# Delta rule, turn and gated sum as one program ordered by keys

## The chip, the cores and the metric

The kernel runs on one core of one Trainium2 chip. The metric is device time in microseconds (us) for one launch. The core's engines are TensorE (PE in the profile, PEld its weight loads), VectorE (DVE), ScalarE (ACT), GpSimd (POOL) and SyncE (SP), which issues most transfers; each works through its own list of instructions in order and waits on semaphores.

## What is computed

One step of a hybrid decoder layer for 512 prompt tokens and 8 sample tokens that share the weights. The part in question, cut from the reference:

```python
proj = einsum('btd,df->btf', u, w_in)            # u = rmsnorm(x)
o_nsa, o_mem = ...                               # two attention mixers
o_gdn, s_new = gated_delta_chunked(q, k, v, g, beta, s0)
o_gdn = rmsnorm(o_gdn, o_norm) * silu(z)
gates = sigmoid(g_br)                            # g_br: 3 x 1024 columns of u @ w_in
merged = (gates[:, :, 0] * (o_nsa @ w_br_nsa)
          + gates[:, :, 1] * (o_gdn @ w_br_gdn)
          + gates[:, :, 2] * (o_mem @ w_br_mem))
h = x + merged @ w_out
y = h + square(relu(rmsnorm(h) @ w_ff1)) @ w_ff2
```

For a sample token the delta rule is one step on a 128x128 state per head and sequence (32 states): read k·S and q·S, form the new value, and S becomes e^g·S + k·v'.

## The kernel before

The kernel is a list of stages, `stages()`. Each is one block in which every engine gets its instructions; at a block's end the engines meet at a barrier. Semaphores made with `local_sem` are cleared and freed between stages (`retire`, L222) with a further barrier; those made with `sem` live to the end. The last stages are:

- `stage_gdn_sample`: the sample tokens' delta rule. SP loads the 32 states (`s_S`, 2 MB) and the first two weight tiles. DVE and PE go through a chain: norms of q and k (L2350 to L2364), 32 small products that read the states (L2318, each shows as two matmuls of 2 columns), new value `s_vn` and result `s_oT` (L2371 to L2377), two transposes to rows (L2321, L2322), four of the result (L2325), then the norm and gate of the result into `proj` (L2382 to L2389). The states' update is eight products of 512 columns (L2331); DVE scales a quarter head pair (L2393) and adds the product (L2395). SP stores the states and waits for the stores.
- `stage_turn`: the three mixers' results, in `proj` by tokens, are turned to channels by PE (L2441, 15 groups of four transposes) and split by DVE into a high part `oH` and a low part `oL` (`high_low`, L298 and L300), so that one fp32 product is three float32r products. SP loads back the input `u` as `uH` and `uL` (2 MB each).
- `stage_merge`: 12 pairs of weight tiles of 256 columns. A gate tile (1024 rows, 1 MB) gives four units of 24 matmuls, whose sum ACT takes through a sigmoid (L2512) into `sig`. The branch tile that follows it (512 rows, 0.5 MB) gives four units of 12 matmuls, which DVE multiplies with `sig` (L2527) and, from the second branch on, adds to `mergedT` (L2532, L2534); in the last four pairs it also splits the sum (L298, L300). Gate units take turns in PSUM banks 0 to 3, branch units in 4 to 7. DVE splits every tile, `split_tile`, as soon as PE has done the tile two before it; two buffers each for raw, high and low weights. At its end it splits the first two tiles of `w_out`, and SP loads `h` (the input x, 2 MB).
- `stage_out_ffn`: output product with `w_out` (four tiles, units of 24 matmuls over token tiles, added to `h` at L2735), norm, and the feed-forward network (L329 under L2588). A unit waits until the sum of the unit four before it is taken from its bank.

All products go through `product3` (L329), so this line is that of most matmuls. `by_key` merges several generators into one list of instructions: each yields a number before a piece of code, and the piece with the lowest number is written next. It sets the order on an engine; what is waited for is set by the semaphores.

Of the kernel before, what the change touches and what calls it, by code (L numbers as in the profile page):

```python
# [69 lines left out]
def rows(t):  # L70
    return P if t < TT else NB
# [98 lines left out]
class Kernel:  # L170
# [73 lines left out]
    def build(self):  # L244
        nc = self.nc
        with self.stack:
# [17 lines left out]
            self.vecs_loaded = self.sem("vecs_loaded")  # L264
            stages = self.stages()
# [441 lines left out]
    def stage_inputs(self):  # L707
# [81 lines left out]
        self.beta, self.g = self.sb("beta", [P, TT + 1, GH]), self.sb("g", [P, TT + 1, GH])  # L789
# [715 lines left out]
    def stage_prompt_mixers(self):  # L1505
# [14 lines left out]
        self.cTs = self.sb_high("cTs", [P, CC, NB])  # L1520
# [749 lines left out]
    def stage_gdn_sample(self):  # L2270

        nc, I, O, ps, proj = self.nc, self.I, self.O, self.ps, self.proj
        ident, cTs = self.C("ident"), self.cTs
        HB = GH * NB
        S0 = self.sb("s_S0", [P, GH, NB, P])
        self.wt = [self.sb(f"wt{i}", [P, KC, WCOLS]) for i in range(2)]
        sq, qkn = self.sb("s_sq", [P, 2 * HB]), self.sb("s_qkn", [P, 2 * HB])
        rn = self.sb("s_rn", [P, 2 * HB])
        pairs = self.sb("s_pairs", [P, HB, 2])
        prod = self.sb("s_prod", [P, HB])  # L2280
        gb = self.sb("s_gb", [NB, 2, HB])
        bcs = self.sb("s_bcs", [P, 3, HB])
        vn, oT = self.sb("s_vn", [P, HB]), self.sb("s_oT", [P, HB])
        rows_kv = self.sb("s_rows", [HB, 2, P])
        Vm = self.sb("s_Vm", [HB, HB, P])
        eg = self.sb("s_eg", [NB, GH])
        tmp = self.sb("s_tmp", [P, HB])
        so, sqo = self.sb("s_so", [NB, GH]), self.sb("s_sqo", [NB, GH, GD])
        S = self.sem
        s_in, stored = S("s_in"), S("s_stored")  # L2290
        p = Steps(S("s_pe"), ["sums", "bc", "qk", "read", "rows", "orow"] + [f"add{i}" for i in range(8)])
        a = Steps(S("s_act"), ["eg", "rt", "rows", "sqo", "ro"])
        v = Steps(S("s_dve"), ["sq", "mean", "gb", "prod", "pairs", "vn", "oT", "Vm", "so", "out"] + [f"add{i}" for i in range(8)])
        two = lambda x: x.rearrange("p c b -> p (c b)")
        with nc.Block() as block:
            @block.sync
            def _(sp):
                for h in range(GH):
                    sp.dma_start(S0[:, h], I["state_gdn"][:, h].rearrange("b k v -> k b v")).then_inc(s_in, 16)
                for srcs, chunks in self.merge_tiles()[0:2]:  # L2300
                    self.load_tile(sp, srcs, chunks)
                for h in range(GH):
                    v.wait(sp, f"add{2 * h + 1}", 0)
                    sp.dma_start(O["s_state"][:, h].rearrange("b k v -> k b v"), S0[:, h]).then_inc(stored, 16)
                sp.wait_ge(stored, 64)

            @block.tensor
            def _(pe):
                v.wait(pe, "sq", 0)
                p.done(pe.matmul(ps[:, 0, 0:2 * HB], self.C("ones"), sq[:, :], start=True, stop=True), "sums", 0)  # L2310
                v.wait(pe, "gb", 0)
                p.done(pe.matmul(ps[:, 1, 0:2 * HB], self.C("ones")[0:NB, :], gb.rearrange("b i c -> b (i c)"), start=True, stop=True), "bc", 0)
                v.wait(pe, "prod", 0)
                p.done(pe.matmul(ps[:, 2, 0:HB], self.C("ones"), prod[:, :], start=True, stop=True), "qk", 0)
                v.wait(pe, "pairs", 0)
                pe.wait_ge(s_in, 64)
                for i in range(HB):
                    ins = pe.matmul(ps[:, 3, 2 * i:2 * i + 2], S0[:, i // NB, i % NB, :], pairs[:, i, :], start=True, stop=True)  # L2318
                p.done(ins, "read", 0)
                v.wait(pe, "vn", 0)  # L2320
                pe.transpose(ps[0:HB, 4, 0:P], qkn[:, HB:], ident)  # L2321
                p.done(pe.transpose(ps[0:HB, 4, P:2 * P], vn[:, :], ident), "rows", 0)  # L2322
                v.wait(pe, "oT", 0)
                for h in range(GH):
                    ins = pe.transpose(ps[0:NB, 5, h * P:(h + 1) * P], oT[:, h * NB:(h + 1) * NB], ident)  # L2325
                p.done(ins, "orow", 0)
                v.wait(pe, "Vm", 0)
                for i in range(8):
                    if i >= 2:
                        v.wait(pe, f"add{i - 2}", 0)  # L2330
                    p.done(pe.matmul(ps[:, 6 + i % 2, :], rows_kv[:, 0, :], Vm[:, 4 * i:4 * i + 4, :], start=True, stop=True), f"add{i}", 0)  # L2331

            @block.scalar
            def _(act):
                a.done(act.activation(eg[:, :], self.g[0:NB, TT, :], ACT.Exp), "eg", 0)
                v.wait(act, "mean", 0)
                a.done(act.activation(rn[:, :], rn[:, :], ACT.Sqrt), "rt", 0)
                p.wait(act, "rows", 0)
# [513 lines left out]
```

## Time and profile before

| | us |
|---|---|
| median of 3 runs | 1685.5 (1683.55 to 1691.86) |
| the profiled execution, its own time | 1689.1 |
| span of that execution | 1687.2 |
| PE, PEld, DVE, ACT, POOL busy | 1472.1, 1348.7, 880.0, 374.7, 82.0 |
| mean granted TensorE clock, share of full speed | 0.907 |

The profile is of one execution, whose own time stands beside its span. Times in its rows are microseconds from the span's start, and a row that ends in `[idle before <-releaser]` tells how long the engine had done nothing and what ended that. The three stages that the change joins reach from 950.4 to 1241.3.

### The profile page before, as it was taken

The numbers are of one execution on the slowest core, as the hardware profiler recorded it, in microseconds if no ns is written. First come the engines' busy times: TensorE is split into PE (matmuls) and PEld (weight loads), VectorE is DVE, ScalarE is ACT, GpSimd is POOL, SyncE is SP. The second block draws the span as 40 slices with busy tenths as digits, with TensorE's granted clock in tenths as the row PEclk, the third lists the DMA queues.
The fourth block names the chain that finished last, engine by engine and source line by source line (L and its number), as shares of the span: only waits on it lengthen the run. The fifth ranks groups of instructions, "written<-read, shape, count | busy, mean of one in ns | idle before, by whom it ended". The sixth has DMA issues, their size and how long they took to land. (4 is left out here: it accounts for less than half of the span.)

```text
span 1687.2 us, 27010 instructions
## 1 busy us (share of the span) xinstructions
PE 1472.1 (87%) x11343; PEld 1348.7 (80%) x11343; DVE 880.0 (52%) x1598; ACT 374.7 (22%) x874; POOL 82.0 (5%) x76
## 2 busy tenths in 40 slices
PE   6999899879878788988556567999989999999998
PEld 5778789879877677867344447999979999999998
DVE  3554257658434556654233264445654746555563
ACT  3543033223314344544122100010003101000000
POOL 0000001100011111110000000000000000000000
PEclk8999999989958798988678658999989999999999
DMA  9231125142401000000754342332341233233231
GB/s 342 87 131 59 50 79 179 51 175 79 132 10 51 0 1 1 1 1 8 302 204 156 97 149 77 92 96 77 99 164 38 75 101 100 79 97 99 75 101 51
DMA packets 115649, 159.03 MB, mean 94 GB/s; under 512 B 6040, under 2 KB 106840, under 8 KB 112779
## 3 DMA queue, kind: packets, MB, share of 16 engines
q1 hardware_dynamic: 111886, 122.76, 22.7%
q0 software_dynamic: 2304, 33.56, 4.9%
q8 instruction: 84, 1.38, 0.4%
q10 hardware_dynamic: 1348, 1.12, 0.2%
q14 instruction: 27, 0.21, 0.0%
HBM read 145.04 MB, written 16.66 MB: 96 GB/s over the span
## 5 line engine op out<-in xcount | busy, mean ns | idle before, releaser
L329 PE MATMUL ps<-uH,wh 128*128 128x260 f32 x576 | 165.5, 287 | 21.3 <-DVE wl L300 12.4
L298 DVE CAST wh<-wt 128x2048 fp32r<-128x2048 f32 (+1 forms) x75 | 85.7, 1143 | 128.7 <-PE ps L329 101.0
L329 PE MATMUL ps<-hH,wh 128*128 128x260 f32 x512 | 145.6, 284 | 2.6 <-DVE hT L300 2.6
L329 PE MATMUL ps<-mergedH,wh 128*128 128x260 f32 x512 | 145.5, 284 | 0.0
L329 PE MATMUL ps<-hH,wl 128*128 128x260 f32 x512 | 145.5, 284 | 0.0
L329 PE MATMUL ps<-hT,wh 128*128 128x260 f32 x512 | 144.8, 283 | 0.0
L329 PE MATMUL ps<-mergedH,wl 128*128 128x260 f32 x512 | 144.6, 282 | 0.0
L329 PE MATMUL ps<-mergedT,wh 128*128 128x260 f32 x512 | 144.6, 282 | 0.0
L456 PE MATMUL ps<-XT,w 128*128 128x256 f32 (+1 forms) x512 | 125.7, 387 | 6.3 <-DVE XT L519 6.0
L329 PEld LDWEIGHTS ps<-uH,wh 128*128 128x128 f32 x576 | 110.6, 192 | 21.6 <-issue 12.5
L300 DVE TENSOR_TENSOR wl<-wt,wh 128x2048 fp32r<-128x2048 f32 (+1 forms) x58 | 120.2, 2072 | 2.0
L329 PE MATMUL ps<-uL,wh 128*128 128x260 f32 x384 | 109.7, 286 | 0.0
L329 PE MATMUL ps<-uH,wl 128*128 128x260 f32 x384 | 109.6, 285 | 0.0
L456 PEld LDWEIGHTS ps<-XT,w 128*128 128x128 f32 x512 | 92.8, 192 | 19.1 <-DVE XT L519 7.4
L329 PEld LDWEIGHTS ps<-hH,wh 128*128 128x128 f32 x512 | 97.2, 190 | 2.8 <-DVE hT L300 2.8
L329 PEld LDWEIGHTS ps<-hT,wh 128*128 128x128 f32 x512 | 97.1, 190 | 0.0
L329 PEld LDWEIGHTS ps<-hH,wl 128*128 128x128 f32 x512 | 97.0, 189 | 0.0
L329 PEld LDWEIGHTS ps<-mergedH,wh 128*128 128x128 f32 x512 | 96.4, 188 | 0.0
L329 PEld LDWEIGHTS ps<-mergedH,wl 128*128 128x128 f32 x512 | 96.4, 188 | 0.0
L329 PEld LDWEIGHTS ps<-mergedT,wh 128*128 128x128 f32 x512 | 96.4, 188 | 0.0
L2721 ACT ACTIVATE positive<-ps 128x260 f32<-128x260 f32 x64 | 24.9, 389 | 300.7 <-PE ps L329 300.7
L329 PE MATMUL ps<-wh,uH 128*128 128x256 f32 (+1 forms) x304 | 87.8, 289 | 0.0
(517 smaller groups left out, 3427.3 us busy)
## 6 DMA issues: line engine op xcount, KB each, us to landing
wt<-in_w_ff SPq DMA_DIRECT2D x32, 1024.0 KB, 5.3
wt<-in_w_in SPq DMA_DIRECT2D x27, 1024.0 KB, 5.4
ring<-in_cache_mem_kv SPq DMA_DIRECT2D x4, 2048.0 KB, 25.1
w<-in_cmp_w SPq DMA_DIRECT2D x8, 512.0 KB, 7.8
ring<-in_cache_win_kv SPq DMA_DIRECT2D x2, 2048.0 KB, 19.5
wt<-in_w_out SPq DMA_DIRECT2D x4, 1024.0 KB, 6.1
out_s_win<-in_cache_win_kv SPq DMA_DIRECT2D x1, 4088.0 KB
scratch_uhigh<-uH SPq DMA_DIRECT2D x1, 2080.0 KB
```

The lines of the kernel that those rows point to most:

```text
L298: dve.tensor_copy(high, x).then_inc(high_sem, 1)
L300: return dve.tensor_tensor(low, x, high.bitcast(F32), ALU.subtract)
L329: ins = pe.matmul(out, lhsT(i, c), rhs(j, c), start=(first and c == 0 and k == 0), stop=(last and c == chunks - 1 and k == 2))
L456: return pe.matmul(out, self.w1[:, v, J * r + j, :], x, start=(i == 0), stop=(i == 2 * J - 1))
L2721: act.activation(positive[:, k % 4, :], ps[:, k % 4, 0:HALF], ACT.Relu).then_inc(relu, 1)
```

## The change

`stage_gdn_sample`, `stage_turn` and `stage_merge` become one block, `stage_tail`, whose five lists are written with `by_key`. What it does:

- The order of tiles is gate 0, gate 1, then branch q and gate q + 2 in turn; it ends gate 11, branch 10, branch 11. `sig` holds two tiles. Gate units have banks 0 and 1, branch units 2 to 4, early turns 2 to 5, the delta rule 6 and 7.
- 14 of the 15 groups of transposes stand ahead of the first product or right behind it; the sample rows of the delta rule's mixer, which need its result, come in the third gate tile. ACT now makes `oH`, DVE makes `oL`.
- The small products, transposes and state updates of the delta rule stand between units. `Vm` is made in eight parts of 512 columns instead of one of 4096.
- SP issues the first weight tile, `uH`, `uL`, the second tile, the states, then the rest. Three raw buffers; the low part of a tile is written over its raw part, so tile n is loaded when tile n - 3 is done.
- `h` is loaded, and the second tile of `w_out` split, at the start of `stage_out_ffn`. The new stage's semaphores are local, so that `retire` stands behind it.

```diff
-    def stage_turn(self): ...
-    def stage_merge(self): ...
+    def stage_tail(self):
...
+        seq = [("gate", 0), ("gate", 1)]
+        for q in range(Q):
+            seq += [("branch", q)] + ([("gate", q + 2)] if q + 2 < Q else [])
...
+        START = 13.0
+        start = [START]
+        for kind, _ in seq:
+            start.append(start[-1] + NU * (2.87 if kind == "gate" else 1.44))
+        unit_at = lambda n, i: start[n] + i * (start[n + 1] - start[n]) / NU
...
+        turns = [(br, t) for br in range(3) for t in range(TT)] + [(0, TT), (2, TT), (1, TT)]
+        EARLY = len(turns) - 1
+        turn_key = lambda i: 1.5 + 1.1 * i if i < EARLY else 47.0
...
+        add_key = lambda i: 49.0 + 6.0 * i
...
+                def load(n):
...
+                    if n >= 3:
+                        sp.wait_ge(self.w_split, k - 1)
+                        sp.wait_ge(acc, self.tile_end[k - 3])
...
+                def loads():
...
+                    load(0)
+                    for x, dram in zip((self.uH, self.uL), self.u_dram):
+                        sp.dma_start(x.bitcast(F32)[:, :, :], dram).then_inc(u_back, 16)
+                    load(1)
+                    for h in range(GH):
+                        sp.dma_start(S0[:, h], I["state_gdn"][:, h].rearrange("b k v -> k b v")).then_inc(s_in, 16)
...
+                            if kind == "gate":
+                                if u >= 2:
+                                    pe.wait_ge(gated, u - 1)
+                                out, rhs, chunks = ps[:, u % 2, 0:HALF], lambda i, c: X[i][:, c, tok], KC
+                            else:
+                                if u >= 3:
+                                    pe.wait_ge(taken, u - 2)
+                                out, rhs, chunks = ps[:, 2 + u % 3, 0:HALF], lambda i, c: O3[i][:, q // BP, c, tok], 4
...
+                    for i in range(HB):
+                        if i % 8 == 0:
+                            yield 26.0 + 3.0 * (i // 8)
...
+                    for i in range(8):
+                        yield add_key(i) + 1.0
...
+                def splits():
+                    yield 6.5
+                    split(0)
+                    for n in range(1, NT_ + 1):
+                        yield start[n - 1] + 0.2
+                        split(n)
...
     def stage_out_ffn(self):
...
+                sp.dma_start(h[:, 0:TT, :], I["x_prompt"][0].rearrange("(t p) d -> p t d", p=P)).then_inc(h_in, 16)
+                sp.dma_start(h[0:NB, TT, :], I["x_sample"][:, 0, :]).then_inc(h_in, 16)
...
+                self.high_low(dve, self.last_raw, self.wh[k % 2], wlow[k % 2], self.w_high, k + 1).then_inc(self.w_split, 1)
...
-                dve.wait_ge(self.h_in, 32)
+                dve.wait_ge(h_in, 32)
```

Where it moves instructions, first on PE at the start of the joined stages, as far as the first product. Before (`s_S` are the states, `proj` the results to be turned, `consts` the identity or ones, UNCONDITIONAL_BRANCH a block's edge):

```order
L2310 MATMUL ps<-s_sq_9120,consts_49 128x64
L2312 MATMUL ps<-s_gb_9125,consts_49 128x64
L2314 MATMUL ps<-s_prod_9124,consts_49 128x32
L2318 MATMUL ps<-s_pairs_9123,s_S_127_9117 128x2 x32
...
L2325 MATMUL ps<-consts_49,s_oT_9128 8x128 x4
L2331 MATMUL ps<-s_Vm_9130,s_rows_9129 128x512 x8
L2295 UNCONDITIONAL_BRANCH
L2433 UNCONDITIONAL_BRANCH
L2441 MATMUL ps<-consts_49,proj_1644 128x128 x16
...
L329 MATMUL ps<-uH_9336,wh_154_9491 128x260
```

With the change (`temps` are the delta rule's small tiles), with the first unit's 24 matmuls cut short:

```order
L2447 MATMUL ps<-temps_9141,consts_49 128x64
L2440 MATMUL ps<-consts_49,proj_1647 128x128 x4
L2450 MATMUL ps<-temps_9141,consts_49 128x64
L2440 MATMUL ps<-consts_49,proj_1647 128x128 x4
L2453 MATMUL ps<-temps_9141,consts_49 128x32
L2440 MATMUL ps<-consts_49,proj_1647 128x128 x36
L330 MATMUL ps<-uH_9122,wh_144_9134 128x260
...
L2440 MATMUL ps<-consts_49,proj_1647 128x128 x4
L2440 MATMUL ps<-consts_49,proj_1647 128x8 x8
...
L2460 MATMUL ps<-temps_9141,s_S_135_9125 128x2 x8
```

The state reads and updates now stand behind the first product, between units; 11 groups of transposes stand ahead of it, one full and two small groups behind its first unit.

On SP at the same place, before and then with the change:

```order
L2299 DMA s_S_127_9117<-in_state_gdn 128x8x128 x4
L291 DMA wt_128_9118<-in_w_in 128x8x256
L291 DMA wt_129_9119<-in_w_br_nsa 128x4x256
L2304 DMA out_s_state<-s_S_127_9117 128x8x128 x4
L2295 UNCONDITIONAL_BRANCH
L2428 UNCONDITIONAL_BRANCH
L2431 DMA uH_9336<-scratch_uhigh 128x4160
L2431 DMA uL_9337<-scratch_ulow 128x4160
```

```order
L2375 DMA tw_136_9126<-in_w_in 128x8x256
L2382 DMA uH_9122<-scratch_uhigh 128x4160
L2382 DMA uL_9124<-scratch_ulow 128x4160
L2375 DMA tw_137_9127<-in_w_in 128x8x256
L2385 DMA s_S_135_9125<-in_state_gdn 128x8x128 x4
L2375 DMA tw_138_9128<-in_w_br_nsa 128x4x256
```

`uH` and `uL` moved from behind the stores of the states to behind one weight tile, and the states behind both.

On DVE from the end of the joined stages into the next, before:

```order
L298 CAST mergedH_9500<-mergedT_9498 128x260
L300 TENSOR_TENSOR mergedT_9501<-mergedT_9498,mergedH_9500 128x260
L298 CAST wh_156_9493<-wt_129_9119 128x2048
L300 TENSOR_TENSOR wl_160_9497<-wt_129_9119,wh_156_9493 128x2048
L2476 UNCONDITIONAL_BRANCH
L2723 UNCONDITIONAL_BRANCH
L2748 MEMSET ss_12007 128x15
L298 CAST woH_174_11999<-wt_128_9118 128x2048
```

With the change:

```order
L299 CAST mergedH_9139<-mergedT_9138 128x260
L301 TENSOR_TENSOR mergedT_9140<-mergedT_9138,mergedH_9139 128x260
L2364 UNCONDITIONAL_BRANCH
L2839 UNCONDITIONAL_BRANCH
L299 CAST wh_145_9135<-tw_137_9127 128x2048
L301 TENSOR_TENSOR tw_140_9130<-tw_137_9127,wh_145_9135 128x2048
L2868 MEMSET ss_12007 128x15
L299 CAST woH_163_11999<-wt_154_11990 128x2048
```

The second `w_out` tile's split moved from ahead of the block's edge to behind it. `h` and the third `w_out` tile are now issued behind the same edge.

## Rows read from the trace of the kernel before

**Rows 1.** The page, part 1: busy time of each engine, share of the span.

```profile
PE 1472.1 (87%) x11343; PEld 1348.7 (80%) x11343; DVE 880.0 (52%) x1598; ACT 374.7 (22%) x874; POOL 82.0 (5%) x76
```

**Rows 2.** Windows: stretch, its length, busy us of each engine, granted clock, DMA share, GB/s.

```profile
950.40:1023.10 72.70, 40.51 (x152) 28.11 (x153) 41.42 (x74) 4.18 (x7) 0.00 (x0) 0.55 0.43 138
1023.10:1236.00 212.90, 210.13 (x1728) 209.94 (x1728) 104.82 (x157) 18.63 (x48) 0.00 (x0) 0.99 0.33 102
```

**Rows 3.** Timeline of PE, next stage: start, us, engine, line, operation, idle before.

```profile
1241.31 0.55 PE L329 MATMUL ps<-wh,mergedH 128*128 128x256 f32 x1 [8.06 <-PEq L2476]
```

**Rows 4.** Timeline of PE, delta rule to first product, same columns.

```profile
960.92 13.78 PE L2318 MATMUL ps<-s_pairs,s_S 128*128 128x2 f32 x64 [6.71 <-DMA s_S<-in_state_gdn]
...
976.19 1.01 PE L2325 MATMUL ps<-consts,s_oT 128*8 128x128 f32 x4
...
985.71 10.60 PE L2331 MATMUL ps<-s_Vm,s_rows 32*128 32x512 f32 x12 [0.91 <-DVE s_S L2395]
...
1008.96 0.66 PE L2441 MATMUL ps<-consts,proj 128*128 128x128 f32 x4 [0.55 <-DVE oL L300]
...
1023.12 0.56 PE L329 MATMUL ps<-uH,wh 128*128 128x260 f32 x1 [12.42 <-DVE wl L300]
```

**Rows 5.** Transfers issued from 940 to 1060: KB each, us to landing.

```profile
wt<-in_w_in SPq DMA_DIRECT2D x4, 1024.0 KB, 5.3
...
uL<-scratch_ulow SPq DMA_DIRECT2D x1, 2080.0 KB, 13.9
```

**Rows 6.** Windows of 2 us in the turn stage, columns of rows 2.

```profile
1004.00:1006.00 2.00, 2.00 (x19) 1.75 (x19) 1.97 (x4) 0.00 (x0) 0.00 (x0) 0.98 0.98 416
1012.00:1014.00 2.00, 0.00 (x0) 0.00 (x0) 1.90 (x6) 0.00 (x0) 0.00 (x0) 0.50 0.16 67
```

**Rows 7.** Timeline of SP, where the turn stage issues its transfers.

```profile
1000.71 0.34 SPq L2431 DMA_DIRECT2D uH<-scratch_uhigh  x1
```

**Rows 8.** Timeline of DVE in the last pair of tiles and at the next stage's start.

```profile
1220.13 0.69 DVE L298 CAST wh<-wt 128x1024 fp32r<-128x1024 f32 x1
1220.85 1.23 DVE L300 TENSOR_TENSOR wl<-wt,wh 128x1024 fp32r<-128x1024 f32 x1
...
1231.06 0.42 DVE L2532 TENSOR_TENSOR m_prod<-ps,sig 128x260 f32<-128x260 f32 x1
1231.51 0.43 DVE L2534 TENSOR_TENSOR mergedT<-mergedT,m_prod 128x260 f32<-128x260 f32 x1
1231.98 0.30 DVE L298 CAST mergedH<-mergedT 128x260 fp32r<-128x260 f32 x1
1232.31 0.43 DVE L300 TENSOR_TENSOR mergedT<-mergedT,mergedH 128x260 fp32r<-128x260 f32 x1
...
1237.44 1.22 DVE L298 CAST wh<-wt 128x2048 fp32r<-128x2048 f32 x1
1238.69 2.29 DVE L300 TENSOR_TENSOR wl<-wt,wh 128x2048 fp32r<-128x2048 f32 x1
...
1248.19 1.23 DVE L298 CAST woH<-wt 128x2048 fp32r<-128x2048 f32 x1 [6.78 <-DMA wt<-in_w_out]
```

**Rows 9.** Timeline of ACT over the joined stages, same columns.

```profile
950.68 1.28 ACT L2337 ACT_TABLE_LOAD   x1
951.98 0.26 ACT L2337 ACTIVATE s_rn<-s_rn 128x64 f32<-128x64 f32 x1
...
1028.43 0.39 ACT L2512 ACTIVATE sig<-ps 128x260 f32<-128x260 f32 x1 [7.85 <-PE ps L329]
...
1227.52 0.39 ACT L2512 ACTIVATE sig<-ps 128x260 f32<-128x260 f32 x1 [2.50 <-PE ps L329]
```

**Rows 10.** Timeline of DVE, first operation behind a stage whose semaphores are local.

```profile
950.48 0.23 DVE L2350 TENSOR_TENSOR s_sq<-cTs 128x64 f32<-128x64 f32 x1 [1.37 <-PEq L222]
```

**Rows 11.** Windows of 2 us in the next stage, columns of rows 2.

```profile
1310.00:1312.00 2.00, 0.61 (x6) 0.40 (x4) 1.97 (x2) 0.39 (x1) 1.35 (x1) 1.00 0.00 0
1316.00:1318.00 2.00, 2.00 (x11) 2.00 (x10) 1.93 (x5) 0.37 (x1) 0.00 (x0) 0.50 0.09 26
```

More of the change, by code:

```diff
@@ new lines, in loads @@
+                def loads():
+                    yield 0.0
+                    load(0)
[4 more added lines that the diff above has]
+                        sp.dma_start(S0[:, h], I["state_gdn"][:, h].rearrange("b k v -> k b v")).then_inc(s_in, 16)
+                    for n in range(2, len(tiles)):
+                        yield start[n - 2] if n >= 3 else 0.1
+                        if n == 2:
+                            sp.wait_ge(self.w_split, k0 + 1)
+                        load(n)
@@ new lines, in turn @@
+                def turn():
+                    for i, (br, t) in enumerate(turns):
+                        yield turn_key(i)
+                        if i == EARLY:
+                            v.wait(pe, "out", 0)
+                            pe.wait_ge(oL_kept, EARLY)
+                        elif i >= 4:
+                            pe.wait_ge(oL_kept, i - 3)
+                        if (br, t) == (2, TT):
+                            pe.wait_ge(self.mem_back, 16 * MH)
+                        for c in range(4):
+                            ins = pe.transpose(ps[:, turn_bank(i), c * P:c * P + rows(t)], proj[0:rows(t), t, cols[br] + c * P:cols[br] + (c + 1) * P],
+                                               ident[0:rows(t), 0:rows(t)])
+                        ins.then_inc(turned, 1)
@@ new lines, in dense @@
+                def dense():
+                    for n, (kind, q) in enumerate(seq):
+                        if kind == "gate":
+                            continue
+                        for i, (m, tok) in enumerate(U):
+                            yield unit_at(n, i + 1) + 0.1
+                            u = NU * q + i
+                            dst, high, lo = (x[:, WM * (q % BP) + m, tok] for x in (self.mergedT, self.mergedH, self.mergedL))
+                            dve.wait_ge(gated, u + 1)
+                            dve.wait_ge(acc, acc_of("branch", q, i))
+                            if u == 0:
+                                dve.wait_ge(turned, EARLY)
+                            x, y = ps[:, 2 + u % 3, 0:HALF], sig[:, q % 2, m, tok]
+                            if q < BP:
+                                dve.tensor_tensor(dst, x, y, ALU.mult).then_inc(taken, 1)
+                                continue
+                            e = u - BP * NU
+                            if e >= 2:
+                                dve.wait_ge(added, e - 1)
+                            dve.tensor_tensor(prod2[:, e % 2, :], x, y, ALU.mult).then_inc(taken, 1)
+                            dve.wait_ge(taken, u + 1)
+                            dve.tensor_tensor(dst, dst, prod2[:, e % 2, :], ALU.add).then_inc(added, 1)
+                            if q >= 2 * BP:
+                                dve.wait_ge(added, e + 1)
+                                self.split_acts(dve, dst, high, lo)
@@ new lines, in _ @@
+                by_key(splits(), dense(), turn(), sample())
+                dve.wait_ge(self.x_split.sem, self.x_split.n)
+        self.issued, self.splits = k0 + NT_ + 2, k0 + NT_ + 1
+        low_of = {(k0 + NT_ + i) % 2: (NT_ + i) % 3 for i in range(2)}
+        third = (NT_ + 2) % 3
+        self.wl = [low[low_of[i]] for i in range(2)]
+        for i in range(2):
+            self.taken[f"wl{i}"] = self.taken.pop(f"tw{low_of[i]}")
+        self.last_raw = raw[(NT_ + 1) % 3]
+        self.taken["wt0"] = self.taken.pop(f"tw{third}")
```

477 lines of the change are left out of this document (242 added, 235 removed).

## Prediction

> **What bounds the kernel now.** I read the page's table of engines first: PE is busy for 1472.1 of 1687.2 us, DVE for 880.0, so the end moves only if time in which PE has no useful work goes [rows 1]. Then windows by stage. From 1023.1 to 1236.0, the gated sum, PE is busy for 210.1 of 212.9 us at a clock of 0.99: full, 1728 matmuls of 0.122 us. From 950.4 to 1023.1, delta rule and turn, it is busy for 40.5 of 72.7 us at 0.55, near the lower of its two levels (1.2 of 2.4 GHz) [rows 2]; ahead of the next stage's first product, at 1241.31, it stands for 8.06 [rows 3]. The timeline shows what those 72.7 us are: a wait for the states, 13.8 us of state reads at half clock, the updates, then transposes that wait for DVE, and 12.4 us in which PE waits for DVE's last splits, until the first product at 1023.12 [rows 4]. That product needs `uH`, `uL` and one split weight tile. None of the delta rule is needed before the second branch, so the stretch is a queue of things that stand ahead of the product only by the order of stages.
>
> **The start.** S is 950.4. The first product now waits for the later of two things.
> - Transfers. Before, `uL` landed 13.9 us after it was issued [rows 5]; the traffic of it and `uH` (4.26 MB) ran at 416 GB/s and had almost ended at 1012.4, 11.7 us after the first issue at 1000.7 [rows 6, 7]. Now one tile of 1.05 MB goes ahead, 2.5 us at 416 GB/s. So 11.7 + 2.5 = 14.2 at the low end, and 0.4 + 13.9 + 2.5 + 0.7 = 17.5 at the high end. I take 16, the middle.
> - DVE and the transposes. The first tile lands at about 5.3 [rows 5]. DVE by then has the short chain of norms (some 4 us) and four turns; it splits at 7.5 to 11 (3.5 us [rows 8]) and turns 4 to 7 follow. The 11th group of transposes needs DVE's seventh turn, so PE is through at about 13.5. ACT's half of a turn runs beside DVE's. This hides under the transfers by 2.5 us; without them it would set the start.
>
> The first product moves from S + 72.7 to S + 16: **56.7 us gained**. The slow clock of its first unit (ended 5.3 us after it began, where units at full clock take 24 x 0.12 = 2.9 [rows 4, 9]) is paid as before.
>
> **What PE gets in between.** It is PE time on the path now, but at full clock, at which a matmul pitch is half.
> - State reads: 13.8 us at 0.50 [rows 4], so 6.9 at full clock; upper bound 13.8.
> - Updates: 12 matmuls, six products, took 10.6, 1.77 each; eight at half of that are 7.1; upper bound 14.1.
> - Transposes of the new value and the result: 1.01 at half clock for four [rows 4], six now: 0.8.
> - The turn groups behind the first product: one full, 0.66 at full clock [rows 4], and three of 8 columns, which I bound by 0 and 0.66 and take as 0.4: 1.9.
>
> Sum **16.7 us lost**, up to 32 if none of it speeds up.
>
> Waits in between: the two transposes to rows stand behind the third unit of branch 0 (4.3 us after its begin). DVE must by then have split gate 2 (3.5), taken a unit (0.43) and made `vn` (0.7): 4.6. So PE waits 0.3. The late turn stands two gate units (5.8) behind the result's transposes; DVE's chain there is a unit 0.4, a small split 1.9, the reduce 0.8, the root 0.2, norm and gate 2.3: 5.6, hidden by 0.2 to 0.7. The eight updates add 16 us of DVE work over some 50 us in which DVE was busy for half; PE's third unit ahead is the cover (three branch banks), and by my walk through the list a unit's bank is free 0.3 us before it is wanted. If that cover goes, each branch tile waits what DVE is late.
>
> ACT now loads tables twice more, between the result's transposes and the third gate tile's first sigmoid. The row shows 1.28 us per load, and the operation behind it starts 0.02 us after its end [rows 9]. The chain square 0.6, load, root at 3.4, load, sigmoid ends at 5.1 after branch 0; PE wants that bank at 6.2. Hidden: 0. The Trainium skill ("ScalarE: Activation LUTs", What ACT_TABLE_LOAD costs) counts a drain of about 1380 ns beside the load's 1283, 2.66 us per switch of set; by that the sigmoid would end at 7.1 and PE would wait 0.9 us. The rows have no such drain, so the sum goes by them.
>
> **The end of the stage.** After the last gate tile there are now two branch tiles. DVE's list from there: a small split 1.9 (0.69 + 1.23), four units of 1.6, a full split 3.5, four units of 1.6 [rows 8]: 18.2 us, against PE's 11.6; DVE ends it. Then 0.4 to the next stage, and 1.0 more since the semaphores are now local: the one such place shows 1.37 us idle [rows 10], where this edge took 0.3 to 0.4 [rows 3, 8]. Together 19.6. Before, from the last gate unit's end at 1227.5 [rows 9] to 1241.3 [rows 3] it was 13.8, with one branch tile. The other tile's 48 matmuls (5.8) have left the part ahead, so the end costs 19.6 - 5.8 = 13.8: **0**. PE's idle time moves, it doesn't go.
>
> **The next stage.** DVE starts with a split of 3.5 us, then waits for `h`, which was loaded long before and is now issued here, 2.1 MB ahead of the third `w_out` tile. That tile was split at 1248.19, 6.9 us behind the edge [rows 3, 8]; 2.1 MB at 416 GB/s add up to 5, so its split begins at 10 to 11.8 and the first sum leaves its bank at 14 to 15.8. PE has four banks: ramp and four units are 2.4 + 4 x 2.85 = 13.8. So it waits 0 to 2 us; **1 lost**. The 16 splits of `oH` that went to ACT and the rest of DVE's savings lie beside PE: 0.
>
> **Sum.** 56.7 - 16.7 - 0.3 - 0 - 1 = 38.7 us. On this execution's own 1689.1 that is 1650.4; it was 3.6 us above the median of the runs, and on the median of 1685.5 it is 1646.8. I forecast **1647 us**.
>
> **Rivals.**
> 1. *The start comes later.* The second tile (1.05 MB) and the states (2.1 MB) are issued right behind `uL` and share the engines. With all 8.5 MB at 300 to 416 GB/s before the last piece of `uL` lands, the first product is at S + 26. For it: `uL` landed 2.6 us after the traffic's end. Against it: `uH` and `uL` ran at nearly full share of the engines, and what is issued first mostly lands first. 10 us less gain: **1657**. Chance 0.14.
> 2. *The pieces between units stay dear.* Each switch from product to small matmul and back waits for a semaphore, and the reads keep their half-clock price: 15 us less, **1662**. For it: only rows at the low clock show them. Against it: the transposes at 0.66 for four ran at full clock within a stretch of small ones. Chance 0.09.
> 3. *Slower: the clock.* PE stood for some 2.6 us around 1312, and by 1316 its granted clock was 0.50 [rows 11]; a fall costs 2.4 us as in the first unit. Gate units have two banks instead of four, branch units three. If PE stands that long at the 23 tile edges, it pays 55 us: 1647 + 55 = **1702**. It decides from 16 falls (38.7 / 2.4). Against it: a sigmoid takes 0.39 us and has a whole unit of 2.9 us of cover, and a split of 3.5 us has a tile of 5.8. Chance 0.03. The Trainium skill ("TensorE: Matmul & The Clock Gate", A second HAM failure mode: psum-queue depth-cycling) says that small idle times between groups of matmuls, from cycling through PSUM banks, make the clock fall and rise again and again. By that rule the result would be this rival's; the trace of before, at 0.99 over the gated sum, does not show it with four banks.
> 4. *The change doesn't do what it says*: some wait in one of the five lists keeps the product behind the delta rule, and only the store wait and the stage edges go, some 8 us: 1678. Chance 0.02.
>
> **Numbers.** My forecast has 0.72 (own range 1640 to 1653: start 14.2 to 17.5, next stage 0 to 2, runs of before 6 us apart). Rivals 0.14, 0.09, 0.03, 0.02. The range 1640 to 1660 holds most of the forecast, rival 1 and part of rival 2, some 0.82. A measurement can tell about 0.5%, 8.4 us, from no change. Faster by more: forecast, rivals 1 and 2, 0.95; within: 0.02; slower: 0.03.
>
> **What would show it.** The first product with `uH` 16 us after the first small matmul of the delta rule; state reads of some 1.7 us for eight; updates of 0.9 us; a clock of 0.98 or more from there to the last gate tile; PE idle for 6 to 8 us at the edge; `h` and the third `w_out` tile landing 10 us behind it. Wrong: a first product later than S + 20, idle times of PE over 1 us at tile edges, or a clock under 0.95 in the gated sum.

## The result and the profile after

The changed kernel takes 1650.17 us in the median of 4 runs (1644.59 to 1651.61), the kernel before beside it 1688.68 (4 runs). The ratio is 0.977, with an interval of 0.9743 to 0.9796: 38.5 us less. The forecast was 1647, the range 1640 to 1660. In a later set of six executions the ratio was 0.9782 (0.9748 to 0.9817). One execution of the combined version further down, at 2105.31 us and a granted clock of 0.637, was in a slower state of the chip and is left out of its median.

The page's table of engines, of the changed kernel's profiled execution (own time 1644.59, span 1642.8, clock 0.929):

```profile
PE 1453.0 (88%) x11343; PEld 1335.0 (81%) x11343; DVE 871.7 (53%) x1590; ACT 384.5 (23%) x891; POOL 82.1 (5%) x76
```

PE has the same 11343 matmuls as in [rows 1] and is busy for 19.1 us less. Of these, 12.6 lie in the joined stages (250.6 to 238.1), where work of the slow clock now runs at the fast one, and 5.8 lie ahead of them, in code that is the same. The span is 44.4 us shorter, so the other 25.3 were idle time of PE. But 44.4 is more than the change gives, as a cut of each execution at three marks shows: the first DVE operation of the joined stages (S), the next stage's first product, and the end.

| us | before S | S to next stage's first product | from there to the end |
|---|---|---|---|
| before | 950.5 | 290.8 | 445.9 |
| changed | 942.9 | 252.8 | 447.1 |
| changed, profiled again | 956.5 | 252.7 | 447.1 |

The stretch before S, whose code is the same in both kernels, lies up to 13.6 us apart in two executions of one and the same kernel; the other two repeat to 0.1 in these two. So single executions are compared by the second and third columns: 290.8 - 252.8 = 38.0 gained in the stage, 1.2 lost behind it, 36.8 in all.

The third column is less firm than the second. In the experiments that leave the order of tiles and the next stage's code alone it lies between 444.9 and 447.8. Most of that is PE's clock: 74 us into the next stage PE stands for 2.6 us in every one of these executions, and behind it the clock falls in some and not in others. The windows right behind that idle time, in the changed kernel and in a run of the experiments (length, busy us of PE, its weight loads, DVE, ACT, POOL, granted clock, DMA share, GB/s):

```profile
1269.50:1273.00 3.50, 3.50 (x17) 3.50 (x18) 3.47 (x3) 0.00 (x0) 0.00 (x0) 0.51 0.00 0
```

```profile
1276.60:1280.10 3.50, 3.48 (x29) 3.48 (x30) 3.47 (x3) 0.29 (x1) 0.00 (x0) 1.00 0.00 0
```

PE does 17 matmuls in the one and 29 in the other. A fall like this costs about 1.5 us, twelve matmuls of 0.12. So a difference of 1 or 2 us behind the stage, the 1.2 among them, isn't the edit's for certain.

Now the places that the prediction spoke of. PE's timeline, at the first product and then the small work between products (start, us, engine, line, operation, idle before and what ended it):

```profile
953.92 1.91 PE L2440 MATMUL ps<-consts,proj 128*128 128x128 f32 x12 [3.40 <-DVE oL L2570]
959.15 0.56 PE L330 MATMUL ps<-uH,wh 128*128 128x260 f32 x1 [3.32 <-DMA uL<-scratch_ulow]
...
985.63 1.84 PE L2460 MATMUL ps<-temps,s_S 128*128 128x2 f32 x16
...
996.40 0.27 PE L2464 MATMUL ps<-consts,temps 128*32 128x128 f32 x1
...
998.05 0.60 PE L2469 MATMUL ps<-consts,temps 128*8 128x128 f32 x4
1004.34 0.41 PE L2440 MATMUL ps<-consts,proj 8*128 8x8 f32 x4
...
1007.55 0.28 PE L330 MATMUL ps<-uH,tw 128*128 128x260 f32 x1
1007.76 1.12 PE L2477 MATMUL ps<-temps 32*128 32x512 f32 x2
1008.82 0.38 PE L330 MATMUL ps<-uH,wh 128*128 128x260 f32 x1
1009.04 0.28 PE L330 MATMUL ps<-uL,wh 128*128 128x260 f32 x1
```

S is 942.94. The first product stands at S + 16.2 where it was at S + 72.7 [rows 2, 4], and what it waits for last is `uL`. The reads, which took 13.8 us in one piece at half clock [rows 4], are four groups of 1.84. The row of 1004.34 is the late turn: no idle time ahead of it. The last four rows are an update between two products. From the start of the last product before it to the start of the second behind it are 1.49 us, where two products in a row take 0.24: an update costs 1.25 us, more than its row's 1.12. All waits of PE in the stage and at its edge, but for one of 6.0 us that lies mostly ahead of S, from the view of waits (us in total, times, longest):

```profile
PE ps L330 <- PEq L222: 5.5, 1, 5.5
PE ps L2440 <- DVE oL L2570: 3.4, 1, 3.4
PE ps L330 <- DMA uL<-scratch_ulow: 3.3, 1, 3.3
PE ps L330 <- DVE m_prod L2557: 2.2, 1, 2.2
PE ps L330 <- DVE h L2851: 1.8, 1, 1.8
```

Two lie ahead of the first product (`oL`, `uL`), two at the stage's end (`m_prod` and the edge, L222), one in the next stage (`h`); between the first product and the last gate tile there is none, none for `sig` and none for `wh` or `wl` either. The windows say the same (columns as above):

```profile
942.90:959.10 16.20, 9.20 (x50) 7.72 (x50) 12.15 (x24) 7.91 (x14) 0.00 (x0) 0.71 0.95 365
959.10:976.30 17.20, 17.15 (x133) 16.99 (x134) 6.83 (x8) 3.59 (x8) 0.00 (x0) 0.90 0.78 200
976.30:1060.00 83.70, 83.70 (x638) 76.26 (x637) 43.52 (x65) 10.09 (x22) 0.00 (x0) 1.00 0.31 91
1060.00:1176.30 116.30, 116.30 (x970) 116.30 (x969) 59.22 (x92) 10.52 (x27) 0.00 (x0) 1.00 0.30 91
1176.30:1195.70 19.40, 11.72 (x96) 11.31 (x94) 17.31 (x36) 0.39 (x1) 0.00 (x0) 0.97 0.34 109
```

In the start the DMA engines are at 0.95 and PE works 9.20 of 16.20 us; behind it PE is full up to 1176.3, at full clock once the first unit's matmuls of 0.42 us are over at 962.4; in the end part PE works 11.72 of 19.40 us and DVE 17.31.

DVE's timeline from the edge into the next stage:

```profile
1195.75 1.23 DVE L299 CAST wh<-tw 128x2048 fp32r<-128x2048 f32 x1 [1.17 <-PEq L222]
...
1207.58 1.23 DVE L299 CAST woH<-wt 128x2048 fp32r<-128x2048 f32 x1 [8.26 <-DMA wt<-in_w_out]
1208.84 2.29 DVE L301 TENSOR_TENSOR woL<-wt,woH 128x2048 fp32r<-128x2048 f32 x1
1211.05 1.41 DVE L2851 TENSOR_TENSOR h<-h,ps 128x256 f32<-128x256 f32 x4
```

The edge costs 1.17 us of idle time, where it was 0.3 to 0.4 [rows 8]. DVE then stands for 8.26 us for the third `w_out` tile, and the first sum starts at 1211.05, 15.3 behind the edge, with PE's four banks full. The chain of waits goes through the same place: `w_out` issued at 1196.58, in the chain for 10.90 us, the two splits, the sum, and then PE's products.

ACT, where it loads tables once more each for the root and the sigmoid:

```profile
999.30 1.28 ACT L2515 ACT_TABLE_LOAD   x1
1001.42 0.21 ACT L2515 ACTIVATE temps<-temps 8x4 f32<-8x4 f32 x1 [0.84 <-DVE temps L2610]
1001.65 1.28 ACT L2492 ACT_TABLE_LOAD   x1
1002.94 0.39 ACT L2492 ACTIVATE sig<-ps 128x260 f32<-128x260 f32 x1
```

### The profile page after: what moved, and what is told of

Same layout as the page of the kernel before. It is cut to its first block and busy times, and to the rows that moved or that the text cites. A ratio compares the mean times of both kernels' runs of the same rounds, so it can differ in the third digit from the quotient of the medians.

```text
span 1642.8 us, 27036 instructions
## 1 busy us (share of the span) xinstructions
PE 1453.0 (88%) x11343; PEld 1335.0 (81%) x11343; DVE 871.7 (53%) x1590; ACT 384.5 (23%) x891; POOL 82.1 (5%) x76
## 3 DMA queue, kind: packets, MB, share of 16 engines
q8 instruction: 84, 1.38, 0.4%
q10 hardware_dynamic: 1348, 1.12, 0.2%
## 5 line engine op out<-in xcount | busy, mean ns | idle before, releaser
L330 PE MATMUL ps<-uH,tw 128*128 128x260 f32 x384 | 109.0, 284 | 0.0
L457 PEld LDWEIGHTS ps<-XT,w 128*128 128x128 f32 x512 | 92.7, 192 | 19.1 <-DVE XT L520 7.4
L2837 ACT ACTIVATE positive<-ps 128x260 f32<-128x260 f32 x64 | 24.9, 389 | 299.9 <-PE ps L330 299.9
L330 PE MATMUL ps<-wh,uT 128*128 128x256 f32 (+1 forms) x304 | 85.7, 282 | 0.0
L330 PE MATMUL ps<-wt,uH 128*128 128x256 f32 (+1 forms) x304 | 85.5, 281 | 0.0
## 6 DMA issues: line engine op xcount, KB each, us to landing
ring<-in_cache_win_kv SPq DMA_DIRECT2D x2, 2048.0 KB, 19.5
```

The lines of the kernel that those rows point to most:

```text
L330: ins = pe.matmul(out, lhsT(i, c), rhs(j, c), start=(first and c == 0 and k == 0), stop=(last and c == chunks - 1 and k == 2))
L457: return pe.matmul(out, self.w1[:, v, J * r + j, :], x, start=(i == 0), stop=(i == 2 * J - 1))
L2837: act.activation(positive[:, k % 4, :], ps[:, k % 4, 0:HALF], ACT.Relu).then_inc(relu, 1)
```

## The experiments

All are edits of the changed kernel. Each ran once, with a profile, but for the last pair, which ran six times each. What is compared is the stage's length from S (252.8 in the changed kernel), since the stretch before S moves by itself.

### The order of the stages put back

```diff
-        START = 13.0
+        START = 100.0
```

All products get keys behind all of the delta rule, with everything else of the change in place.

> One block as in the change, but the numbers of the products start at 100 instead of 13, so that the whole delta rule stands ahead of the first product on every engine. In the change the first product is 16.3 us after the first operation of the joined stage and the stage lasts 252.8 us. Theory (the gain is idle PE time that the products fill): the chain of reads, new value and eight updates at half clock takes the start to 55 to 65 us, the 15 to 17 us of small work leave the part behind it, the stage lasts about 280 us, and only some 10 of the 38 us of gain are left. Rival (the gain is that of fewer stage edges, of the store wait and of ACT's share of the turn): the stage stays within 5 us of 252.8.

Measured: first product S + 63.7, stage 281.1, time 1685.28. The view of waits over the stage has what had been hidden back:

```profile
PE ps L2460 <- DMA s_S<-in_state_gdn: 12.1, 1, 12.1
PE ps L2440 <- DVE proj L2617: 4.2, 1, 4.2
```

So 28.3 of the 38.0 us hang on the products' place ahead of the delta rule. The other 9.7 (290.8 to 281.1) come with everything else: in this kernel no store of the states and no stage edges stand ahead of the turn and of `uH` and `uL`, ACT makes `oH`, and `Vm` comes in parts. The split isn't clean. The states are still issued behind `uH` and `uL`, and with nothing to do meanwhile PE waits for them 5.4 us longer than before (12.1 against 6.7 [rows 4]). With the states issued first, the joining would most likely show more than 9.7 and the order less than 28.3. How the 9.7 divide was not tried.

### The lead of two gate tiles

```diff
-        seq = [("gate", 0), ("gate", 1)]
-        for q in range(Q):
-            seq += [("branch", q)] + ([("gate", q + 2)] if q + 2 < Q else [])
+        seq = [(kind, q) for q in range(Q) for kind in ("gate", "branch")]
```

> Only the order of tiles is undone: gate 0, branch 0, gate 1, branch 1, as before. Theory (PE never waits for a sigmoid with the gates one tile ahead either; the end is DVE's list): no wait of PE over 0.5 us between the first product and the last gate tile; at the end only one branch tile stands behind the last gate tile, so DVE needs 3.5 + 4 x 1.6 = 9.9 us and the edge 1.4 instead of 19.4, of which 5.8 were the other branch tile's products: the stage is 2.3 us shorter, 250.5. Rival (the lead of two tiles is cover that is needed): branch tiles wait for sigmoids or for their weights, 0.5 us or more at each of 12, and the stage is 4 us or more longer.

Measured: stage 251.4, 1.4 shorter than with the lead. The end part is 11.2 us (240.2 to 251.4) instead of 19.4, and one wait is new:

```profile
PE ps L2438 <- DVE proj L2615: 0.9, 1, 0.9
```

It is the late turn, which needs the lead or a later key; no split and no sigmoid came late without the lead. The lead isn't what pays here. In the stage it even costs: with two branch tiles at the end, DVE's 18.2 us of list stand against PE's 11.6. But nothing of the 1.4 us reaches the end of the kernel in this execution: from S it is 700.0 us, where the changed kernel takes 699.9. In the next stage PE waits 2.6 us for `h` instead of 1.8, and its clock falls once more behind that wait. The time, 1657.0, is above the changed kernel's median, since its stretch before S was 12 us longer.

### Gates in one bank

```diff
-                                if u >= 2:
-                                    pe.wait_ge(gated, u - 1)
-                                out, rhs, chunks = ps[:, u % 2, 0:HALF], lambda i, c: X[i][:, c, tok], KC
+                                if u >= 1:
+                                    pe.wait_ge(gated, u)
+                                out, rhs, chunks = ps[:, 0, 0:HALF], lambda i, c: X[i][:, c, tok], KC
```

(and the sigmoid reads that bank.) A gate unit now waits for the sigmoid of the one before: small idle times by design.

> The gate units have one PSUM bank instead of two, so that each of 48 waits for the sigmoid of the one before it. Theory (the cover is the unit of 2.9 us, and small idle times do not lower the clock): each wait is the sigmoid's 0.39 us and two handoffs, 0.5 to 0.6, so the stage is 24 to 30 us longer and the granted clock of the products stays at 0.98 or more. Rival 3 of the prediction (idle times between groups make the clock fall): it falls below 0.9, and the stage is 50 us or more longer.

Measured: stage 277.7, 24.9 longer. The waits, one of them by its neighbours on PE, and the clock over the products (the window's columns as above):

```profile
PE ps L330 <- ACT sig L2492: 17.2, 30, 1.9
```

```profile
977.11 0.28 PE L330 MATMUL ps<-uH,tw 128*128 128x260 f32 x1
977.86 0.39 PE L330 MATMUL ps<-uH,wh 128*128 128x260 f32 x1 [0.48 <-ACT sig L2492]
978.10 0.28 PE L330 MATMUL ps<-uL,wh 128*128 128x260 f32 x1
```

```profile
971.00:1188.00 217.00, 201.14 (x1559) 187.97 (x1559) 96.80 (x144) 22.55 (x53) 0.00 (x0) 1.00 0.30 89
```

PE waits 30 times for a sigmoid, 0.48 us all but twice (1.9), and the clock stays at 1.00. The waiting is the cost: from the last product ahead of such a wait to the second behind it are 0.99 us instead of 0.24, so a wait of 0.48 costs 0.75, and 30 of them, two longer, come to 25 us, as measured. So short idle times at 30 of the 48 gate units do not lower the clock. It is no test of what rival 3 supposed, idle times of some 2.6 us at tile edges; those did not arise in the changed kernel. The Trainium skill ("TensorE: Matmul & The Clock Gate", A second HAM failure mode: psum-queue depth-cycling) tells of short idle times from cycling through PSUM banks that make the clock go down and up again, seen with bf16 matmuls of 512 columns. With the products here, this run does not show it.

### The small work twice

```diff
-                        ins = pe.matmul(ps[:, 7, 2 * i:2 * i + 2], S0[:, i // NB, i % NB, :], pairs[:, i, :], start=True, stop=True)
+                        for _ in range(2):
+                            ins = pe.matmul(ps[:, 7, 2 * i:2 * i + 2], S0[:, i // NB, i % NB, :], pairs[:, i, :], start=True, stop=True)
```

and the same for the updates' outer products.

> Each state read and each of the eight updates' products is issued twice, to the same bank, with the same result. Theory (this work is on PE's path at full clock): 4 x 1.84 us of reads and 8 x 0.9 us of updates more, 14.5 us, all of it in the stage's length: 267. Rival 2 (each switch between product and small work costs as much as the work itself): the same pieces cost less than they do in the change the first time, the increase is 5 to 8 us. Third view (there was slack on PE): under 4 us.

Measured: stage 275.9, 23.1 longer: a miss. The updates were not it: from the transposes of the rows to the last gate unit it took 186.75 us where the changed kernel takes 179.9, 6.85 more, eight times 0.86. The other 16.2 us lie earlier, where the doubled reads should have cost 7.4. The windows there:

```profile
984.00:988.00 4.00, 4.00 (x22) 4.00 (x23) 0.00 (x0) 0.00 (x0) 0.00 (x0) 0.57 0.01 4
...
1004.00:1008.00 4.00, 4.00 (x20) 4.00 (x20) 0.00 (x0) 0.00 (x0) 0.00 (x0) 0.50 0.02 4
...
1016.00:1020.00 4.00, 4.00 (x36) 3.88 (x35) 1.64 (x8) 0.36 (x1) 0.00 (x0) 1.00 0.00 0
```

PE is busy in every one of these microseconds, and still its granted clock is 0.57 and 0.50 in two of them: most of the time at the lower level. Its timeline shows what it did:

```profile
981.47 4.01 PE L2461 MATMUL ps<-temps,s_S 128*128 128x2 f32 x32
...
985.71 0.42 PE L330 MATMUL ps<-uL,wh 128*128 128x260 f32 x1
```

Behind a group of 4.0 us of reads, matmuls of two columns, the products have 0.42 us each instead of 0.28. So a new theory: it isn't idle time that lowers the clock here, it is a long stretch of very narrow matmuls. The reads of before fit it. The windows ahead of them and over them:

```profile
942.70:960.90 18.20, 4.13 (x18) 1.78 (x11) 6.61 (x18) 1.74 (x3) 0.00 (x0) 0.50 0.62 168
960.90:974.70 13.80, 13.78 (x64) 13.72 (x64) 0.00 (x0) 0.00 (x0) 0.00 (x0) 0.50 0.21 67
```

The clock was down before they began, while PE mostly stood, and 13.78 us of reads did not bring it up. The next run tests the theory without doubling anything.

### All reads in one group

```diff
-                        if i % 8 == 0:
-                            yield 26.0 + 3.0 * (i // 8)
+                        if i == 0:
+                            yield 26.0
```

> The 32 state reads (64 matmuls of 2 columns) stand in one group behind the fifth unit instead of in four groups of eight behind units five to eight; nothing else moves and the work is the same. When reads and updates were issued twice, the stage grew by 23.1 us where 14.5 was expected, and the granted clock was 0.50 to 0.58 behind the first double group of 3.8 us. Theory (a longer stretch of these narrow matmuls lets the clock fall though PE is never idle): the group of 7.4 us or more ends at half clock, the products behind it run at 1.2 GHz for some us, and the stage is 3 to 10 us longer than 252.8. Rival (the clock fell by chance of that execution or because of the longer total): the clock stays at 1.00 and the stage within 0.5 us of 252.8.

Measured: stage 258.1, 5.3 longer, with the same instructions. The group and a product behind it, then windows over them:

```profile
985.84 10.51 PE L2460 MATMUL ps<-temps,s_S 128*128 128x2 f32 x64
...
996.57 0.42 PE L330 MATMUL ps<-uL,wh 128*128 128x260 f32 x1
```

```profile
984.00:988.00 4.00, 4.00 (x38) 4.00 (x36) 1.18 (x1) 0.39 (x1) 0.00 (x0) 1.00 0.85 261
988.00:992.00 4.00, 4.00 (x27) 4.00 (x26) 0.00 (x0) 0.00 (x0) 0.00 (x0) 0.66 0.02 5
992.00:996.00 4.00, 4.00 (x21) 4.00 (x20) 0.00 (x0) 0.00 (x0) 0.00 (x0) 0.50 0.00 0
996.00:1000.00 4.00, 4.00 (x21) 4.00 (x22) 0.00 (x0) 0.00 (x0) 0.00 (x0) 0.56 0.00 0
```

PE had been full at 1.00 up to 985.84 and stayed busy; within the group its clock fell. The group takes 10.5 us where four take 7.4, and most of the rest of the 5.3 are products at half clock behind it. The theory holds: that the change puts the reads between products in four groups is worth 5.3 us by itself, beside what it hides. In all nine executions that had the groups of 16, the clock over them is 1.00. Whether it is the two columns that count or something else about these matmuls was not tried.

### The states ahead of everything

```diff
                     yield 0.0
+                    for h in range(GH):
+                        sp.dma_start(S0[:, h], I["state_gdn"][:, h].rearrange("b k v -> k b v")).then_inc(s_in, 16)
                     load(0)
```

(and gone from behind the second tile.)

> SP issues the four loads of the states (2.1 MB) ahead of the first weight tile, uH and uL, nothing else moves. Theory (the transfers up to uL set the start): 2.1 MB at 290 to 300 GB/s are 7 us; the first product moves from 16.3 to 23 us after the stage's first operation and the stage from 252.8 to 259 or 260. Rival (DVE's list sets the start): the first product stays below 18.

Measured: first product S + 23.1, stage 259.6, 6.8 longer. The start goes with the bytes ahead of `uL`: 2.1 MB more cost 6.9 us. The run does not hold DVE's turns still, though: DVE's split waits 6.1 us for the first tile, which is late as well, and PE's last transposes wait 9.6 for the turns behind it. But PE still stands for 3.1 us for `uL` after them.

### `uH` and `uL` in halves

```diff
+                    for half in range(2):
+                        tok = slice(HALF * half, HALF * half + HALF)
+                        for x, dram in zip((self.uH, self.uL), self.u_dram):
+                            sp.dma_start(x.bitcast(F32)[:, :, tok], dram[:, :, tok]).then_inc(u_back[half], 16)
...
+                            if n == 0 and i < 2:
+                                pe.wait_ge(u_back[i], 32)
```

The first unit reads only the first 260 tokens, so it needs half of the bytes.

> uH and uL are loaded in two halves of 260 tokens; the first unit waits for the first half alone. Theory: the first half (2.1 MB) with the tile ahead of it lands at 10 to 12 us after the stage's first operation, and the start is then set by DVE's turns, 13 us (PE was through with the transposes at 955.8, 12.9 us after it): 3 us less, 249.5. Rival (pieces of 1 KB are slower, and the second half is late for the second unit): the first product comes at 13 but the second unit waits, and the stage is as long as in the change.

Measured: first product S + 13.5, stage 250.0, 2.8 shorter. PE's wait for `uL` is gone from the view of waits, and no second unit waited:

```profile
PE ps L2443 <- DVE oL L2573: 3.2, 1, 3.2
```

What sets the start now is PE's own groups of transposes behind DVE's turns, which the prediction had put at 13.5. They ran at half clock in this execution (the last twelve 2.82 us, 1.91 in the changed kernel); in the combined version below, with 1.95, the first product is at 12.6.

### The next stage's sums ahead of both splits

```diff
+                for t in range(UN):
+                    add(0, t)
                 for n in range(2):
                     split_out(n + 2)
-                    for t in range(UN):
-                        add(n, t)
+                for t in range(UN):
+                    add(1, t)
```

> In the next stage DVE takes the first five units out of their banks before it splits the third and fourth tile of w_out, not after the third's split. Theory: PE's wait of 1.8 us ahead of the fifth unit goes, since h lands before the third tile, and nothing waits in its place; from the stage's first product to its 480th matmul it is 1.8 us less. Rival (h lands too late for that as well, or the splits are late for the eleventh unit): a wait of 1 us or more stays, there or at the eleventh unit.

Measured: PE's wait for `h` in the next stage is gone and none took its place; stage 252.5 (unchanged, as it must be), from there to the end 443.6 where it was 447.1, time 1650.32. DVE's timeline:

```profile
1214.26 0.75 DVE L2851 TENSOR_TENSOR h<-h,ps 128x256 f32<-128x256 f32 x2 [5.75 <-DMA h<-in_x_sample]
```

The sums wait for `h` itself, 9.3 us behind the edge at 1204.9, and no longer for the tile behind it and its split of 3.5 us. So the 1.8 us were the order on DVE and not the bytes of `h`. They are only half of the 3.4 by which this part is shorter: this is the run in which the clock did not fall behind the idle time of 2.6 us, and no run shows whether the edit has a share in that.

### What helped, together

Gates and branches in turn, the halves, the sums first, the late turn's key moved from 47 to 55, and the kernel's own semaphores instead of local ones.

> What the runs point to, together: tiles in pairs, the late turn at 55 instead of 47, uH and uL in two halves, DVE's five adds ahead of both splits in the next stage, and the stage's semaphores kept to the end so that no clearing stands behind it. Theory (the terms add, each has its own place on the path): 2.3 for the pairs without the late turn's wait of 0.9, 2.7 for the halves and 1.0 for the edge, so the stage goes from 252.8 to 246.8, and PE's wait of 1.8 to 2.6 behind the next stage's first units goes: 8 us in all. Rival (what one edit frees another takes): a wait of 1 us or more appears where the profile of the change shows none, and the gain is under 5.

Measured: 1638.95, first product S + 12.6, stage 248.4, where 246.8 was expected. The edge costs DVE 0.54 us instead of 1.17. The view of waits has two that weren't counted:

```profile
PE ps L2478 <- issue: 1.1, 1, 1.1
PE ps L330 <- DVE mergedT L2553: 1.0, 1, 1.0
```

Then this version and the changed kernel again, six executions each, beside the kernel before:

> The combined version, timed against the kernel before in five rounds. Its parts in single looks: gate and branch in turn -1.4, halves of uH and uL -2.8, the adds ahead of both splits -1.8, all behind the changed kernel's 1650; a stage of 248.4 us was seen where the changed kernel has 252.8. Theory (the parts add up): about 6 us under the changed kernel, 1644, a ratio of 0.973 to the kernel before. Rival (what the looks gained is scatter of the mixers' stage): the same time as the changed kernel beside it, within 2 us.

> The changed kernel as it is, timed beside the combined version on the same chip. Expected as in its first runs: 1650, a ratio of 0.977 to the kernel before, interval 0.974 to 0.980. Rival: with other runs the stretch before the joined stages falls otherwise and the ratio lies at 0.980 or over.

| | median, us | ratio to before | interval | before S | stage | to the end |
|---|---|---|---|---|---|---|
| changed | 1649.81 | 0.9782 | 0.9748 to 0.9817 | 956.5 | 252.7 | 447.1 |
| combined | 1646.43 | 0.9764 | 0.9727 to 0.9802 | 952.3 | 248.6 | 443.7 |

The last three columns are the profiled execution's. By the times the two can't be told apart: 3.4 us by the medians, 3.0 by the ratios, in intervals 12 us wide, between the rival's 2 and the theory's 6. By the cut, the combined version takes 692.3 us from S to the end, and 692.4 in its first execution, where the changed kernel takes 699.8 and 699.9. So 7.5 us less from S on, repeated to 0.1: 4.1 in the stage, which are the edits', and 3.4 behind it, of which the wait for `h` is 1.8 to 1.9 and the rest goes with the clock. In the times it is hidden by the stretch before S, which lay at 944.8 and 952.3 in two executions of the combined version. Of the two it is the one I would keep, but on the strength of the profile, not of the times.

## Why the prediction was right

- **The start.** 72.7 to 16 forecast, 16.2 measured. That transfers set it and not the turns shows in the wait for `uL` and in two runs: more bytes ahead moved it by 6.9 us, half of the bytes by -2.7, until PE's transposes behind the turns took over at 13.5. PE's wait for `uL`, put at 2.5, was 3.3.
- **Small work.** 16.7 forecast, 19.5 measured: the term that was most mis-sized. Each of the 16 groups between products is measured as the update above. The reads cost 7.1 (6.9 forecast), the transposes and turn groups 2.4 (2.7), the eight updates 1.25 each, 10.0 (7.1). Halving the half-clock price of an update left out what a product behind a group costs more; a second pair of matmuls in the same group costs 0.86, by the doubled run. This is a part of rival 2, 2.8 us of its 15, and it passed unseen in the total. Why the reads came at full clock was only half seen, too. The term took the low clock of [rows 4] for a state that the reads were run in, and that any busy stretch would end. In one group of 64 they bring it down themselves, cost 10.5 us and slow what follows. Rival 2 was a real danger, then, by a mechanism that it didn't name, and the four groups between products are what averts it.
- **The dense stretch** from first product to last gate unit is 217.2 us, where the steps give 198.5 + 16.7 + 0.3 = 215.5. Measured it is 197.7 of products and 19.5 of small work, and no wait. The products are 0.8 shorter than the 198.5 because the first unit is at half clock for 3.3 us, where it was 4.8 before.
- **The wait of 0.3 at the transposes to rows** did not come: 996.40 has no idle time ahead of it.
- **ACT's table loads** cost nothing, as the sum had it. From the result's transposes at 998.05 it is 5.3 us to the sigmoid's end at 1003.33. Each load is 1.28 us and the operation behind the second starts 0.01 after it. Nothing of the drain that the Trainium skill counts beside the load ("ScalarE: Activation LUTs", What ACT_TABLE_LOAD costs) shows, and PE has no wait for `sig`. (The 7.1 that the prediction gives for that rule doesn't follow: as an estimate from that page's 1.38 us, one drain on the 5.1 gives 6.5, two give 7.9.)
- **The stage's end.** 19.6 forecast, 19.4 measured, DVE's list 18.2 with 1.17 at the edge. It is as dear as the prediction said, but it isn't the price of anything: the run with gates and branches in turn shows that the lead buys no cover that is needed, and costs 1.4 us of the stage.
- **The next stage.** 1 forecast (0 to 2), 1.8 measured, by the mechanism named: `h`, the third tile and its split stand ahead of the first sum, 15.3 us behind the edge (14 to 15.8 forecast).

Together: 38.7 forecast; 36.8 from S to the end by the two profiles, 38.5 by the medians. The mechanism was right, and the start, 56.7 forecast and 56.4 measured, carries it. That the medians come within 0.2 us of the sum is luck: the updates were 2.9 too cheap in it, of which smaller terms gave about half back, and the stretch before S, which no edit touches, scatters by more than that. The forecast stood on the median of 1685.5 seen before; one execution more, of 1692.9, moved the median of the kernel before to 1688.68, and that is the 3.2 us between 1647 and 1650.2.

Of the rivals, the later start (1) and the change that does nothing (4) are ruled out by S + 16.2: `uL` was there at 16.2 and the second tile, issued behind it, at 19.1. The slower clock (3) didn't come because its idle times didn't: between the first product and the last gate tile PE has no wait. Rival 2 came in part, as above.

## What to carry to other kernels

When stages are joined, ask which work needs nothing of what stands ahead of it, and let the queue of transfers, not the order of the stages, set when it starts. Small matmuls of a few columns belong between wide ones in short groups; in one long group here, most of them were paid at half clock and the products behind them too. And where an unchanged part of the program scatters by more than an edit is worth, cut each profiled execution at marks on both sides of the edit and compare the pieces.

## What was not expected of the hardware

- **A busy PE at the low clock.** With PE busy in every microsecond and at 1.00 just before, 64 matmuls of two columns in a row brought its clock to 0.50 (10.5 us instead of 7.4), and groups of 32 to 0.50 and 0.57 in windows of 4 us, into the products behind them. Groups of 16 (1.84 us) with 2.9 us of products between them kept 1.00.
- **Short idle times that don't lower it.** 17.2 us of waits in 30 pieces, 28 of them of half a microsecond, left it at 1.00.
- **One idle time, two outcomes.** Behind the same 2.6 us of standing, the clock was 0.51 in one execution and 1.00 in another.
- **The same code at another clock.** The 14 us by which two executions of the changed kernel differ grow mostly between 460 and 700 us, in the mixers (from 2.3 to 13.7). The window of 50 us where they part most, first execution and second:

```profile
550.00:600.00 50.00, 41.78 (x313) 36.84 (x314) 32.03 (x76) 19.18 (x63) 7.63 (x6) 0.90 0.00 1
```

```profile
550.00:600.00 50.00, 40.22 (x243) 35.08 (x243) 27.58 (x66) 15.70 (x47) 7.60 (x6) 0.70 0.00 0
```

PE is about as busy in both, at 0.90 and at 0.70 of full clock, with 313 and 243 matmuls done. What decides it there was not tried.
